# A two-layer hybrid decoder trunk on one core: the end of the DeltaNet mixer put in another order

## The reference

```python
def even_mixer(h, ...):                     # layer 0
    proj = einsum('bsd,de->bse', h, w_in)   # q k v z a b | bg cg xin
    q, k, v = split(silu(causal_conv4(q, k, v)));  q, k = l2_norm(q), l2_norm(k)
    o = gated_delta_rule(q, k, v, g, beta)              # 4 heads of 128
    o = rms_norm(o, o_norm) * silu(z)                   # mixer A, 512 wide ("delta")
    y_sc = bg * causal_conv3(cg * xin)                  # mixer B, 512 wide ("conv")
    return einsum('bse,ed->bsd', concat([o, y_sc]), w_out)

x = x + even_mixer(rms_norm(x, norm1), ...)
x = x + swiglu(rms_norm(x, norm2), w1, w3, w2)          # 1024 -> 3584 -> 1024, dense
# layer 1
x = x + odd_mixer(rms_norm(x, ...), ...)                # sliding-window attention
x = x + moe_swiglu(rms_norm(x, ...), ...)               # 2 of 8 experts, 1024 -> 3584 -> 1024
```

## Time and profile before

| | |
|---|---|
| time, median of 3 runs | 1479.6 us (1478.59 to 1482.23) |
| the profiled execution: its own time | 1479.6 us |
| the profiled execution: span of the trace | 1477.8 us |
| mean granted TensorE clock in it | 0.995 of full speed |
| TensorE busy | 1449.1 us, 98% of the span |
| VectorE busy | 1141.1 us, 77% |
| ScalarE busy | 951.6 us, 64% |
| DMA traffic | 438.77 MB, mean 297 GB/s |

### The profile page before, as it was taken

One profiled execution on the slowest core, in us unless ns is written; L12 is line 12 of the kernel. 1 busy time (PEld: TensorE's weight loads), 2 busy tenths in 40 slices (PEclk: granted clock), 3 DMA queues, 4 the chain that ended last, 5 costly groups with the idle time before them and its releaser, 6 DMA issues.

```text
span 1477.8 us, 19708 instructions
## 1 busy us (share of the span) xinstructions
PE 1449.1 (98%) x7542; PEld 1204.9 (82%) x7542; DVE 1141.1 (77%) x966; ACT 951.6 (64%) x846; POOL 36.2 (2%) x21
## 2 busy tenths in 40 slices
PE   8999999999999999999999999999999999999997
PEld 7988788888886788887888888888888888888886
DVE  6984645544476698888988888898898888889885
ACT  7633544334376667766786777677777777777673
POOL 0000000000000000000000001000000000000000
PEclk9999999999999999999999999999999999999999
DMA  9510746454343399999999999999999999999993
GB/s 350 210 58 4 255 144 254 171 202 167 119 170 128 115 351 385 369 366 371 388 362 395 383 372 367 366 374 378 396 394 371 391 380 357 385 371 380 364 387 124
DMA packets 184239, 438.77 MB, mean 297 GB/s; under 512 B 4864, under 2 KB 6400, under 8 KB 184192
## 3 DMA queue, kind: packets, MB, share of 16 engines
q1 hardware_dynamic: 180496, 426.11, 78.0%
q0 software_dynamic: 2704, 9.96, 2.5%
q10 hardware_dynamic: 992, 2.05, 0.4%
HBM read 431.81 MB, written 6.29 MB: 296 GB/s over the span
## 4 chain that ended last, share of the span: by engine, by line
PE 70%; DMA 10%; issue 9%; DVE 7%; ACT 3%; SPq 0%; DVEq 0%; POOL 0%; ACTq 0%; POOLq 0%
PE ps L268 22%; PE ps L270 22%; PE ps L269 22%; DMA raw<-in_od_moe_w 8%; DVE wlo L257 4%; ACT whi L251 2%; PE ps L446 1%; DMA raw<-in_ev_ffn_w 1%; DMA out<-arena,slot_tok 1%; PE ps L973 1%; PE ps L1171 0%; DVE hTlo L312 0%; PE ps L874 0%; PE ps L2050 0%; ACT arena L1296 0%
## 5 line engine op out<-in xcount | busy, mean ns | idle before, releaser
L257 DVE TENSOR_TENSOR wlo<-raw,whi 128x2048 fp32r<-128x2048 f32 x406 | 906.0, 2272 | 167.3 <-ACT whi L251 164.8
L251 ACT CAST whi<-raw 128x2048 fp32r<-128x2048 f32 x406 | 750.5, 1898 | 245.6 <-DMA raw<-in_od_moe_w 186.8
L268 PE MATMUL ps<-whi,hThi 128*128 128x512 f32 (+1 forms) x1240 | 490.3, 395 | 1.4 <-DVE hTlo L312 1.3
L270 PE MATMUL ps<-whi,hTlo 128*128 128x512 f32 (+1 forms) x1240 | 482.4, 389 | 0.0
L269 PE MATMUL ps<-wlo,hThi 128*128 128x512 f32 (+1 forms) x1240 | 481.8, 389 | 0.0
L270 PEld LDWEIGHTS ps<-whi,hTlo 128*128 128x128 f32 x1240 | 233.2, 188 | 49.3
L268 PEld LDWEIGHTS ps<-whi,hThi 128*128 128x128 f32 x1240 | 233.2, 188 | 49.0 <-issue 2.9
L269 PEld LDWEIGHTS ps<-wlo,hThi 128*128 128x128 f32 x1240 | 233.6, 188 | 46.1 <-issue 0.5
L268 PE MATMUL ps<-whi,aThi 128*128 128x512 f32 x560 | 219.2, 391 | 0.0
L270 PE MATMUL ps<-whi,aTlo 128*128 128x512 f32 x560 | 218.3, 390 | 0.0
L269 PE MATMUL ps<-wlo,aThi 128*128 128x512 f32 x560 | 217.9, 389 | 0.0
(11 more groups left out here) (305 smaller groups left out, 786.2 us busy)
## 6 DMA issues: line engine op xcount, KB each, us to landing
raw<-in_od_moe_w SPq DMA_DIRECT2D x168, 2048.0 KB, 9.9
raw<-in_ev_ffn_w SPq DMA_DIRECT2D x21, 2048.0 KB, 7.8
raw<-in_ev_w_in SPq DMA_DIRECT2D x6, 2048.0 KB, 12.6
raw<-in_ev_w_out SPq DMA_DIRECT2D x2, 2048.0 KB, 8.3
raw<-in_od_w_in SPq DMA_DIRECT2D x2, 2048.0 KB, 7.6
raw<-in_od_w_out SPq DMA_DIRECT2D x2, 2048.0 KB, 8.1
raw<-in_ev_w_in SPq DMA_DIRECT2D x2, 1024.0 KB, 8.5
xres<-in_x SPq DMA_DIRECT2D x2, 512.0 KB, 4.6
```

The lines of the kernel that those rows point to most:

```text
L251: act.copy(whi[s][:, part], raw[s][:, part]).then_inc(hi_ready, 1)
L257: dve.tensor_tensor(wlo[s][:, part], raw[s][:, part], whi[s][:, part].bitcast(F32), ALU.subtract).then_inc(lo_ready, 1)
L268: pe.matmul(to, lhi, rhi, start=first, stop=False)
L270: return pe.matmul(to, llo, rhi, start=False, stop=last)
```

## The change

Five edits to layer 0. Nothing is computed that was not computed before.

1. TensorE's order. The sums of squares of block 0 move ahead of the matmuls of `O[1]`. Then come one conv k-tile of (0,1), the spread of row 0, the sums of squares of block 1, the other three k-tiles of (0,1), the spread of row 1, and the conv part of (1,0). The conv part of (1,1) moves to the very end, behind the four delta parts and behind the turning of the first half of x; the delta part of (1,1) now opens its accumulation and signals a new semaphore `delta_done`. Some PSUM banks are renamed to fit.
2. The second half of `w_out`'s second unit (the k-tiles 4 to 7) is split first on VectorE; the first half is split only behind `mix_lo`.
3. The order of the three first loads of the dense layer: slots 1, 0, 2 where it was 1, 2, 0. The wait for `o_ps` = 2 stands before slot 0's load in both.
4. On VectorE, of unit 10 only the first half is split ahead of the third residual add. The first half of x is split into `hTlo` ahead of the fourth add. The second half of unit 10 is split in the dense layer, behind the second half of x.
5. `up_first` runs k = 0 to 3 of token block 0, then the turning of the second half of x, then k = 0 to 3 of block 1, then k = 4 to 7 of both. Before, the turning stood ahead of all.

```diff
@@ first_loads
-                if order[0] and n == 2:
+                if order[0] and n == 1:
                     sp.wait_ge(o_ps, 2)
@@ even_sync
-            first_loads(sp, U_FFN, ffn_col(w1f), ffn_col(w3f), order=(1, 2, 0))
+            first_loads(sp, U_FFN, ffn_col(w1f), ffn_col(w3f), order=(1, 0, 2))
@@ banks
-        OUT0 = [(ps[3], ps[1]), (ps[2], ps[0])]
-        SUMS, ROWS = ps[5], (ps[7], ps[4])
+        OUT0 = [(ps[3], ps[0]), (ps[1], ps[2])]
+        SUMS, ROWS = ps[7], (ps[5], ps[4])
@@ even_scalar
-            act.wait_ge(gains_in, 16)
-            act.wait_ge(unit_used, U_FFN)
+            act.wait_ge(delta_done, 1)
             act_turned(act, 1, 0)
@@ even_vector
-            split_lo(dve, late, late % NS, halves=(0,))
+            split_lo(dve, late, late % NS, halves=(1,))
             dve.wait_ge(ws_ps, 1)
             dve.tensor_tensor(Vn[:, 1], Vn[:, 1], heads(ps[5]), ALU.subtract).then_inc(vnew_ready, 1)
-            split_lo(dve, late, late % NS, halves=(1,))
...
+            split_lo(dve, late, late % NS, halves=(0,))
             lo_u(dve, U_FFN)
             dve.wait_ge(x_again, 16)
             for n in range(4):
                 if n == 2:
-                    lo_u(dve, U_FFN + 1)
+                    split_lo(dve, U_FFN + 1, (U_FFN + 1) % NS, halves=(0,))
+                if n == 3:
+                    dve_turned(dve, 1, 0)
...
-            dve.wait_ge(gains_in, 16)
-            dve_turned(dve, 1, 0)
@@ project_out
-                pe.wait_ge(lo_ready, 2 * (U_OUT0 + h) + 2)
                 pe.wait_ge(mix_lo, 2)
+                delta_first = (h, t) == (1, 1)
                 for k in ks:
+                    if k == ks[0]:
+                        pe.wait_ge(lo_ready, 2 * (U_OUT0 + h) + (2 if h == 0 or k < H else 1))
@@ even_tensor
+            squares_summed(0)
             pe.wait_ge(vnew_ready, 1)
...
-            squares_summed(0)
+            project_out(0, 1, (H,))
+            spread(4, 5)
             squares_summed(1)
-            project_out(0, 1, conv_part)
-            spread(4, 7)
-            project_out(1, 0, conv_part)
+            project_out(0, 1, (H + 1, H + 2, H + 3))
             spread(5, 4)
-            project_out(1, 1, conv_part)
+            project_out(1, 0, range(H, KD))
             pe.wait_ge(mix_lo, 4)
             for h in range(2):
                 for t in range(TT):
-                    project_out(h, t, delta_part).then_inc((out_ps, unit_used)[t], 1)
-                    if (h, t) == (1, 0):
-                        pe_turn_x(pe, 1, 0)
+                    ins = project_out(h, t, range(H))
+                    ins.then_inc(*((delta_done, 1) if (h, t) == (1, 1) else ((out_ps, unit_used)[t], 1)))
+            pe_turn_x(pe, 1, 0)
+            project_out(1, 1, range(H, KD)).then_inc(unit_used, 1)
@@ dense_vector
             dve_turned(dve, 1, 1)
+            split_lo(dve, u0 + 1, 1, halves=(1,))
             dve_root(dve, 1, link)
@@ dense_tensor
-            pe_turn_x(pe, 1, 1)
...
-            up_first()
+            low, high = range(KD // 2), range(KD // 2, KD)
+            up_first(0, low)
+            pe_turn_x(pe, 1, 1)
+            up_first(1, low)
+            up_first(0, high)
+            up_first(1, high).then_inc(unit_used, 1)
```

More of the change, by code:

```diff
@@ L462, in build_program @@
          m1_ps, m1_ready, upd_ps, T_ready, B_ready, u_ps, u_ready, s1_ps, s1_ready, ws_ps, vnew_ready,
-         o_ps, o_sq, o_ssq, o_ms, o_rt, mix_ready, mix_hi, mix_lo, x_ps, x_ready, b_ps, B_last, z_half) = sem(
+         o_ps, o_sq, o_ssq, o_ms, o_rt, mix_ready, mix_hi, mix_lo, x_ps, x_ready, b_ps, B_last, z_half, delta_done) = sem(
             "pads wab_hi wab_lo ab_done proj_taken gates_in gates_exp g_ready gc_ps "
@@ L467, in build_program @@
             "m1_ps m1_ready upd_ps T_ready B_ready u_ps u_ready s1_ps s1_ready ws_ps vnew_ready "
-            "o_ps o_sq o_ssq o_ms o_rt mix_ready mix_hi mix_lo x_ps x_ready b_ps B_last z_half")
+            "o_ps o_sq o_ssq o_ms o_rt mix_ready mix_hi mix_lo x_ps x_ready b_ps B_last z_half delta_done")
         PROJ = [ps[4:6], ps[6:8], ps[0:2]]
         O = [ps[4], ps[6]]
-        OUT0 = [(ps[3], ps[1]), (ps[2], ps[0])]
-        SUMS, ROWS = ps[5], (ps[7], ps[4])
+        OUT0 = [(ps[3], ps[0]), (ps[1], ps[2])]
+        SUMS, ROWS = ps[7], (ps[5], ps[4])
         ab_chan = ar(9400 + KD * 2 * H, T)[0:2 * H]
@@ L935, in project_out @@
                 wh, wl = band(whi[s], KD, GW), band(wlo[s], KD, GW)
-                pe.wait_ge(lo_ready, 2 * (U_OUT0 + h) + 2)
                 pe.wait_ge(mix_lo, 2)
+                delta_first = (h, t) == (1, 1)
                 for k in ks:
+                    if k == ks[0]:
+                        pe.wait_ge(lo_ready, 2 * (U_OUT0 + h) + (2 if h == 0 or k < H else 1))
                     ins = product(pe, OUT0[h][t][:, :], hThi[:, k, tok], hTlo[:, k, tok], wh[:, k], wl[:, k],
-                                  k == H, k == H - 1)
+                                  k == (0 if delta_first else H), k == (KD if delta_first else H) - 1)
                 return ins
@@ L1009, in even_tensor, with squares_summed @@
             ins.then_inc(ws_ps, 1)
+            def squares_summed(t):
+                pe.wait_ge(o_sq, t + 1)
+                for h in range(H):
+                    ins = pe.matmul(SUMS[:, t * H + h:t * H + h + 1], osq[:, t, h * P:h * P + P], ones[:, 0:1],
+                                    start=True, stop=True)
+                ins.then_inc(o_ssq, 1)
+            squares_summed(0)
             pe.wait_ge(vnew_ready, 1)
@@ L1015, in even_tensor @@
             ins.then_inc(o_ps, 1)
-            def squares_summed(t):
-                pe.wait_ge(o_sq, t + 1)
-                for h in range(H):
-                    ins = pe.matmul(SUMS[:, t * H + h:t * H + h + 1], osq[:, t, h * P:h * P + P], ones[:, 0:1],
-                                    start=True, stop=True)
-                ins.then_inc(o_ssq, 1)
-            conv_part, delta_part = range(H, KD), range(H)
-            squares_summed(0)
+            project_out(0, 1, (H,))
+            spread(4, 5)
             squares_summed(1)
-            project_out(0, 1, conv_part)
-            spread(4, 7)
-            project_out(1, 0, conv_part)
+            project_out(0, 1, (H + 1, H + 2, H + 3))
             spread(5, 4)
-            project_out(1, 1, conv_part)
+            project_out(1, 0, range(H, KD))
             pe.wait_ge(mix_lo, 4)
@@ L1151, in up, with up_first @@
                 ins.then_inc(unit_used, 1)
-            def up_first():
+            def up_first(t, ks):
                 wh, wl = band(whi[0], KD, GW), band(wlo[0], KD, GW)
[L1156 to L1164, removed]
+                tok = slice(t * P, t * P + P)
+                for k in ks:
+                    if k % 2 == 0:
+                        pe.wait_ge(lo_ready, 2 * u0 + k // 4 + 1)
+                        pe.wait_ge(hT_ready, 4 + k // 2 + 1)
+                    ins = product(pe, H1[t][:, :], hThi[:, k, tok], hTlo[:, k, tok], wh[:, k], wl[:, k],
+                                  k == 0, k == KD - 1)
+                return ins
             def turn(i, banks=H1):
```

## The result

The changed kernel took 1467.68 us (median of 5 runs, 1467.11 to 1473.28), the kernel before 1479.6 us: a ratio of 0.9939 with a 95% interval of 0.9915 to 0.9964. Both intervals lie clear of 1; the second comparison has the more runs and is the one to quote.

The account below looks back on a forecast made before the run. TensorE, busy 1449.1 of 1477.8 us, was taken to set the pace. Terms 0.78 - 0.1 + 1.29 + 1.70 + 2.95 - 0.35 = 6.3 us, so 1479.6 - 6.3 = 1473.3 us, range 1470.8 to 1477.6.

Parts of the forecast that it names:

- The layout of TensorE's order: TensorE from the w·S product to the dense layer, new order laid out with old durations: 6.3 us gained.
- The load of unit 9: Dense layer's load issued when O[1] is done: takes 7.8 us instead of 14.15, lands at 154.1, hidden by 3 us.
- rival 2's wide form: Unit 9's load still takes 14.15 us: gain 1.8, 1477.8 us; rival 2 had 0.17, mostly its narrow form.
- The one new hole: TensorE waits 0.35 us for the second row, ahead of the second spread.
- What is late next: Unit 10's second half, the norm's root, unit 11's rounding and load: none within 4 us of the path.
- from the seam's gain to the time: Whole program: the 6.3 us gained before the dense layer reach the end whole, 1479.6 - 6.3 = 1473.3 us.
- run-to-run spread of 1 to 2 us: Whole program's time: part of the allowance by which the range reaches below the forecast.
- 9 us of holes in 1290: TensorE from 180 to 1470 us: busy 1280.75 of 1290 us; idle time there expected unchanged.
- the term that was put at nothing: Behind the seam: TensorE's idle time stays unchanged, so nothing is added to the 6.3 us.
- The clock's term: TensorE's 12 conv matmuls at 148.98 to 153.40 us: 1.70 us gained if the clock stays up; trusted least.
- rival 1: The clock falls once anyway between 143 and 177 us, costing 1.70: gain 4.6, 1475.0 us; chance 0.22.
- rival 3: Clock stays down from 143 us to the dense layer, projection's 84 matmuls take twice as long: 1492 us; chance 0.04.

Follow-up runs that it names:

- e3: Changed kernel with only the edits up to mix_lo, the seam's end as before: 1475.1 us, 0.9965 of the kernel before.
- e4: Changed kernel with only the edits behind mix_lo; sums, spreads, halves of unit 8 and load order as before: 1477.37 us, 0.9997 of the kernel before.
- e7: Changed kernel with the halves of unit 8 split in the old order: 1474.89 us in its one run.
- e8: Changed kernel with the second turning of x ahead of all of up_first: 1471.22 us in its one run.
- e6: Changed kernel with the old order of the dense layer's first loads (slots 1, 2, 0): 1486.31 us, 1.0047 of the kernel before.
- e10: Changed kernel with the conv part of (1,1) ahead of the delta parts and the first turning behind the third of them: 1483.18 us in one run.
- e9: Kernel before with every load of an expert's weight unit cut to its first half, that computation not done: 1475.56 us.
- e5: Changed kernel with every load of an expert's weight unit cut to its first half, that computation not done: 1467.65 us.
- e1: Kernel before, run and traced again without any edit: 1478.92 us (median of 12).
- e2: Changed kernel again without edit, eight runs beside 31 of the kernel before (the second comparison): 1472.09 us, 0.9956 (0.9938 to 0.9974).
- e11: Kernel before with expert loads cut to half and five extra matmuls filling TensorE's hole between the two groups of sums: 1475.58 us.
- e12: Kernel before with only the edits behind mix_lo, and expert loads cut to half: 1474.9 us.

## Why the prediction was right at the seam and wrong in the time

- *The layout of TensorE's order.* Right: 6.3 worked out, 6.4 measured between the cuts in the first pair of traces. The two halves of the change alone (3.4 and 0.7 forecast in e3 and e4, 3.7 and 0.5 measured) and the edits undone in e7 and e8 came within 0.3 us of it. e6's wait was 1.7 us shorter than worked out, and e10 missed by the clock alone (1.93 us of wait for 2.0).
- *The load of unit 9.* Right: 7.8 us and not 14.15; rival 2's wide form did not come, and e6 shows what it costs when this load stands behind another one and is issued late.
- *The one new hole*, 0.35 ahead of the second spread: about 0.2 in the trace (the spread begins at 148.95, the last matmul ahead of it at 148.49).
- *What is late next.* Right: nothing. The stretch to the experts is 333.0 to 333.3 us in every trace, whatever the seam took.
- *The step that failed: from the seam's gain to the time.* The prediction took the 1479.6 us of one execution, subtracted 6.3, and allowed a "run-to-run spread of 1 to 2 us" below. The three runs that it had already lay 3.6 us apart (1478.59 to 1482.23). The experts' stretch scatters from 943.5 to 955 us with the same code in it, mostly for loads that land late; with half loads, where none is late, the medians are 1475.6 and 1467.7 (e9 and e5). The execution that the sum stood on had 4 us of such lateness; three of the five runs of after, at 1467.1 to 1467.7, can have had next to none. The prediction even had the row, 9 us of holes in 1290, and counted it as a fixed property of the kernel instead of asking what the holes were: 2.8 us of it lay in the experts. Of the 12.1 us between the two traces 6.4 are the change; 4.1 are late loads and 1.7 a low clock at another place, both chance. So the term that was put at nothing is what differs outside the seam, and it measured 5.8 us. The range has a slip as well: it was to reach to the 1477.8 of a slow load and ends at 1477.6.
- *The clock's term.* Right for the pair of traces, since the change takes away the low clock and every hole behind it. As a term by itself it was mis-sized: with the clock up at the sums, before waits 1.1 us longer at the seam's end (e1), so the low clock alone cost it about 0.6 us, and in e1 the clock falls at these holes and the seam is 2.7 us longer. Whether the seam of before is dearer than 45.0 us on the average isn't shown: the 7.9 us between e9 and e5 are 1.5 more than 6.4, but e9's trace has 1.7 us ahead of the seam. That the clock would not fall in after was right in all three traces of its seam (after, e2, e5), so rival 1 did not happen in them.
- *What brings the clock down.* The Trainium skill's rule on the clock and idle waits (TensorE: Matmul & The Clock Gate, "HAM oscillation — how this bites in real kernels") is borne out better than I had it. The holes at the seam's end, which I held against it as 2.95 us (2.2 by the idle times of the rows), have the low clock at them in e1 and e11, and a single hole of 1.93 us has it in e10. It is not so in every trace: e3 has 0.85 + 1.30 us of holes there and no fall. In the traces with the order of before at the end, the clock fell there with 3.4 us of holes (e1, e11) and not with 2.2 or 2.4 (before, e3, e9). Whether the longer holes brought it there was not tested, and why the clock fell at the sums in the first trace of before and not in e1 was not settled.
- *Slower by the clock* (rival 3) did not happen. Only e6 comes near: a granted clock of 0.51 from 168.5 to 179, in and behind 11 us of idling.

That the late loads are caused by something in the memory system rather than by this kernel was not tried; e5 and e9 show only that they vanish when half the bytes are moved.

## What to carry to other kernels

The gain at this seam could be worked out to some tenths of a microsecond from one trace, but for the clock, if the order is laid out instruction by instruction for the engine that sets the pace and every wait is checked for its other side. The time of the whole program could not: ask of each remaining hole elsewhere whether it is the kernel's or that execution's, and compare traces between cuts that both have before believing a total. And where work is used as cover for a wait, saving it for a later hole pays only after the first wait is gone: the two edits are worth more together (6.4) than apart (3.7 and 0.5). The reverse also holds: time won ahead of a wait is lost again in the wait, as far as the other side does not move (e11).

## What the runs showed of the hardware

- The experts' loads of 2 MB, issued back to back at 370 GB/s, land late: ScalarE waits up to 6.4 us for one (e10), and TensorE then stands near 700, 800, 815 or 940 us in several traces. With 1 MB each and 189 GB/s there is no such wait. The runs' range falls from 9.3 us (e2) to 1.5 (e5) for the changed kernel, and from 11.1 (e1) to 2.8 (e9) for the one before; in e11 and e12, with half loads too, it is 5.3 and 4.9.
- A stretch at 1.2 GHz costs time on top of the idle time ahead of it: 1.7 us behind a hole of 1.25 (before), 1.8 behind one of 1.93 (e10, 42.3 for 40.5). With one hole filled, the clock fell at the next ones, some 27 us later, which had grown from 2.4 to 3.35 us (e11 beside e9).
